# Weaving three weight slabs by token tile at each layer-norm boundary, and moving two weight and stream transfers to SyncE's queue

## The reference

```python
for l in range(DEPTH):                       # 2 layers
    proj = x @ w_in[l]                       # 1024 -> 5400 columns, feeds three mixers
    y_ssm, y_pool, y_nsa = ...               # state-space scan, causal pooling, sparse attention
    branch_d = einsum('bskc,kcd->bskd', branches, w_branch[l])
    merged = sum(sigmoid(br_g) * branch_d, axis=2)
    x = layer_norm(ALPHA * x + merged @ w_out[l], ln_g[l, 0], ln_b[l, 0])
    h_gate, h_up = split(x @ ffn_w_in[l], 2, axis=-1)
    x = layer_norm(ALPHA * x + (silu(h_gate) * h_up) @ ffn_w_out[l], ln_g[l, 1], ln_b[l, 1])
```

## Time and profile before

| what | value |
|---|---|
| median of three runs | 1762.86 us (1762.06 to 1764.96) |
| the profiled execution's own time | 1763.78 us |
| its span, first to last instruction | 1762.0 us |
| PE busy | 1731.0 us, 98% of the span |
| DVE / ACT / POOL busy | 53% / 37% / 7% |
| mean granted TensorE clock | 0.998 of full speed |
| DMA, mean | 99 GB/s |

### The profile page before, as it was taken

One profiled execution on the slowest core, in us unless ns is written; L12 is line 12 of the kernel. 1 busy time (PEld: TensorE's weight loads), 2 busy tenths in 40 slices (PEclk: granted clock), 3 DMA queues, 4 the chain that ended last, 5 costly groups with the idle time before them and its releaser, 6 DMA issues.

```text
span 1762.0 us, 26801 instructions
## 1 busy us (share of the span) xinstructions
PE 1731.0 (98%) x10172; PEld 1408.2 (80%) x10172; DVE 940.7 (53%) x1514; ACT 650.5 (37%) x1152; POOL 128.2 (7%) x252
## 2 busy tenths in 40 slices
PE   7999999999999999999999999999999999999998
PEld 7778777788888888888887777777888888888886
DVE  5788777545354444422358877865453544444223
ACT  4333666422242222221353346664222522222112
POOL 4710000000000000000047000000000000000000
PEclk9999999999999999999999999999999999999999
DMA  7543111122422222222263331111233222222222
GB/s 261 165 110 89 54 49 49 59 98 100 165 72 96 95 95 96 100 95 92 97 242 117 107 88 60 43 49 67 93 118 118 84 96 95 95 95 95 96 96 84
DMA packets 65918, 174.88 MB, mean 99 GB/s; under 512 B 14256, under 2 KB 26576, under 8 KB 65056
## 3 DMA queue, kind: packets, MB, share of 16 engines
q1 hardware_dynamic: 40192, 140.53, 23.2%
q10 hardware_dynamic: 21888, 13.64, 3.2%
q0 software_dynamic: 3744, 19.41, 3.1%
HBM read 162.27 MB, written 7.08 MB: 96 GB/s over the span
## 4 chain that ended last, share of the span: by engine, by line
PE 92%; DVE 4%; DVEq 2%; ACT 1%; issue 1%; DMA 0%
PE ps L532 20%; PE ps L534 19%; PE ps L533 19%; PE ps L570 6%; PE ps L572 6%; PE ps L571 6%; PE ps L857 2%; PE ps L844 2%; PE ps L830 2%; PE ps L550 1%; PE ps L673 1%; PE ps L561 1%; PE ps L551 1%; PE ps L552 1%; DVE wlo L1376 1%; PE ps L833 1%
## 5 line engine op out<-in xcount | busy, mean ns | idle before, releaser
L532 PE MATMUL ps<-xh,whi 128*128 128x512 f32 x1312 | 520.7, 397 | 5.7 <-DVE wlo L1376 3.4
L534 PE MATMUL ps<-xh,wlo 128*128 128x512 f32 x1312 | 512.0, 390 | 0.0
L533 PE MATMUL ps<-xl,whi 128*128 128x512 f32 x1312 | 511.5, 390 | 0.0
L1376 DVE TENSOR_TENSOR wlo<-raw,whi 128x1024 fp32r<-128x1024 f32 x264 | 324.1, 1228 | 348.4 <-ACT whi L977 339.1
L977 ACT ACTIVATE whi<-raw 128x1024 fp32r<-128x1024 f32 x264 | 278.7, 1056 | 349.2 <-PE ps L572 234.2
L532 PEld LDWEIGHTS ps<-xh,whi 128*128 128x128 f32 x1312 | 246.7, 188 | 57.4 <-DVE wlo L1376 5.1
L534 PEld LDWEIGHTS ps<-xh,wlo 128*128 128x128 f32 x1312 | 246.6, 188 | 52.6
L533 PEld LDWEIGHTS ps<-xl,whi 128*128 128x128 f32 x1312 | 247.0, 188 | 49.1 <-issue 0.5
L570 PE MATMUL ps<-whi,hh 128*128 128x512 f32 x352 | 137.5, 391 | 0.0
L572 PE MATMUL ps<-whi,hl 128*128 128x512 f32 x352 | 137.0, 389 | 0.0
L571 PE MATMUL ps<-wlo,hh 128*128 128x512 f32 x352 | 137.0, 389 | 0.0
(11 more groups left out here) (338 smaller groups left out, 2331.2 us busy)
## 6 DMA issues: line engine op xcount, KB each, us to landing
raw<-wstream SPq DMA_DIRECT2D x264, 512.0 KB, 3.2
w<-w1s POOLq DMA_DIRECT2D x4, 2048.0 KB, 11.7
sm<-smalls POOLq DMA_DIRECT2D x2, 1060.0 KB, 7.1
xt<-xin ACTq DMA_DIRECT2D x4, 512.0 KB, 6.4
scratch_u<-pa ACTq DMA_DIRECT2D x8, 256.0 KB
toep<-scratch_k ACTq DMA_DIRECT2D x4, 512.0 KB
toep_b<-scratch_k ACTq DMA_DIRECT2D x4, 512.0 KB
xt<-xin POOLq DMA_DIRECT2D x4, 512.0 KB, 4.1
```

Source lines behind the costliest of these rows:

```text
L532: pe.matmul(ps[:, bank, :], wh, hi[:, k, :], start=first and i == 0, stop=False)
L533: pe.matmul(ps[:, bank, :], wh, lo[:, k, :], start=False, stop=False)
L534: m = pe.matmul(ps[:, bank, :], wl, hi[:, k, :], start=False, stop=last and i == len(blocks) - 1)
L1376: dve.tensor_tensor(wlo[:, c % 2, :], raw[:, c % 2, :], whi[:, c % 2, :].bitcast(f32), SUB).then_inc(lo_ready, 1)
```

## The change

The last three slabs of an output stage, b-2, b-1 and b, are woven by tile, where it was two. PE's order is now: the three slabs for t = 0, 1; the three for t = 2; b-2 for t = 3; `turn_back` of the first half; b-1 and b for t = 3. Slab b and the next stage's first two slabs b+1, b+2 are split into three new buffers `whi_end`, `wlo_end`, laid over the start of `gates`/`hh`, so they no longer wait for the two ordinary slots; the new stage's third and fourth slabs, b+3 and b+4, are split inside `ln_part` too. `first_pair` starts when both its slabs are split, turns the second half in the middle of the second slab, and alternates the two slabs on the second token half. Layer 0 keeps its old start (`first_slabs`). In the norm DVE normalizes columns 0-511 in both halves, and takes the statistics of tile 3 after three of the four groups of `halves`. The w1 load is cut into 8 pieces of 512 KB per layer, and with the save of x (4 x 512 KB) it is issued by SP between the slab loads of the layer's first slabs instead of by POOL.

```diff
+    whi_end = place("whi_end", big_at, [P, 3, 1024], f32r)
+    wlo_end = place("wlo_end", big_at + 3072, [P, 3, 1024], f32r)
...
-            with sp.Fori(0, L * NSLAB // 2 - 1) as h:
...
+            def load_w1(l, m):
+                j, part = m // 4, slice(1024 * (m % 4), 1024 * (m % 4) + 1024)
+                sp.dma_start(w1[:, j, part], w1s[l * 2 + j, :, part]).then_inc(w1_in[j], 16)
+            for l in range(L):
+                for c in range(8):
+                    load_slab(l * NSLAB + c, c % 2)
+                    if c == 2 and l:
+                        sp.wait_ge(ln_x, l * 16)
+                    if c in (2, 3) and l:
+                        for t in (2 * c - 4, 2 * c - 3):
+                            sp.dma_start(scr_x[:, t, :], xt[:, t, :]).then_inc(x_stored, 16)
+                    if c == 3:
+                        sp.wait_ge(slab_done, l * NSLAB + 4)
+                    if c in (3, 4, 5, 6):
+                        load_w1(l, 2 * c - 6)
+                        load_w1(l, 2 * c - 5)
+                with sp.Fori(0, NSLAB // 2 - 4 - (l == L - 1)) as h:
...
-                if l:
-                    wait(slab_done, l * NSLAB + 2)
-                    load_w1()
-                if l:
-                    wait(ln_x, l * 16)
-                    for t in range(4):
-                        pool.dma_start(scr_x[:, t, :], xt[:, t, :]).then_inc(x_stored, 16)
...
-                if l == 0:
-                    wait(slab_done, 4)
-                    load_w1()
...
+                for s in range(3):
+                    pe.wait_ge(lo_ready, b - 2 + s + 3)
+                    for t in (0, 1):
+                        m = token_products(ends[s][0], ends[s][1], 1, t, k + 2 * s, hi, lo, s == 2)
+                        if s == 2:
+                            m.then_inc(t_psum, 1)
+                for s in range(3):
+                    m = token_products(ends[s][0], ends[s][1], 1, 2, k + 2 * s, hi, lo, s == 2)
+                m.then_inc(t_psum, 1)
+                token_products(ends[0][0], ends[0][1], 1, 3, k, hi, lo, False).then_inc(slab_done, 1)
                 turn_back(n, 0, rt)
-                token_products(b % 2, 1, 3, k + 2, hi, lo, True).then_inc(slab_done, 1)
+                for s in (1, 2):
+                    token_products(ends[s][0], ends[s][1], 1, 3, k + 2 * s, hi, lo, s == 2).then_inc(slab_done, 1)
...
             def first_pair(n, at, rt):
-                pe.wait_ge(lo_ready, at + 3)
+                pe.wait_ge(lo_ready, at + 4)
                 for g in range(4):
                     x_quarter(at, 0, g, n * 8)
-                if n:
-                    turn_back(n - 1, 1, rt)
-                pe.wait_ge(lo_ready, at + 4)
+                for g in (0, 1):
+                    x_quarter(at + 1, 0, g, n * 8)
+                turn_back(n - 1, 1, rt)
+                for g in (2, 3):
+                    x_quarter(at + 1, 0, g, n * 8)
                 for g in range(4):
-                    x_quarter(at + 1, 0, g, n * 8)
-                for c in range(2):
-                    for g in range(4):
+                    for c in range(2):
                         m = x_quarter(at + c, 1, g, n * 8)
...
+            def split_end_hi(c, slot, free):
+                act.wait_ge(raw_loaded[c % 2], (c // 2 + 1) * 16)
+                act.wait_ge(slab_done, free + 3)
+                act.activation(whi_end[:, slot, :], raw[:, c % 2, :], ACT.Copy).then_inc(hi_ready, 1)
+            def stage_splits(at, pairs, last):
+                b = at + 2 * pairs - 1
+                split_end_hi(b, 0, b - 3)
+                if not last:
+                    split_end_hi(b + 1, 1, b - 3)
...
                 for t in (2 * half, 2 * half + 1):
-                    for fh in (0, 1) if half and n < 2 * L - 1 else (1,):
```

More of the change, by code:

```diff
@@ L592, in to_tokens @@
                     residual(n, fh)
-                    for s in range(pairs - 2 * fh):
+                    for s in range(pairs - 3 * fh):
                         c = at + fh * pairs + s
@@ L598, in to_tokens @@
                         for t in range(4):
-                            m = token_products(c % 2, fh, t, 2 * s, hi, lo, fh == 0 and s == pairs - 1)
+                            m = token_products(whi[:, c % 2, :], wlo[:, c % 2, :], fh, t, 2 * s, hi, lo, fh == 0 and s == pairs - 1)
                         m.then_inc(slab_done, 1)
-                a, b = at + 2 * pairs - 2, at + 2 * pairs - 1
-                k = 2 * pairs - 4
-                pe.wait_ge(lo_ready, a + 3)
-                for t in (0, 1):
-                    token_products(a % 2, 1, t, k, hi, lo, False)
@@ new lines, in to_tokens @@
+                ends = ((whi[:, (b - 2) % 2, :], wlo[:, (b - 2) % 2, :]), (whi[:, (b - 1) % 2, :], wlo[:, (b - 1) % 2, :]), (whi_end[:, 0, :], wlo_end[:, 0, :]))
+                k = 2 * pairs - 6
+                for s in range(3):
[4 more added lines that the diff above has]
+                            m.then_inc(t_psum, 1)
@@ L1014, in ln_part @@
                 if not last:
-                    split_hi(0, next_slab)
+                    split_end_hi(next_slab + 1, 2, next_slab - 4)
                 for g in range(4):
                     gained(n, 0, g, rt, last)
+                if not last:
+                    split_next_hi(next_slab + 2, next_slab - 2)
                 deviations(n, 1)
-                if not last:
-                    split_hi(0, next_slab + 1)
                 normalized(n, 1, rt)
@@ L1023, in ln_part @@
                     gained(n, 1, g, rt, last)
+                if not last:
+                    split_next_hi(next_slab + 3, next_slab - 2)
             def x_part(buf, q):
@@ L1344, in _ @@
                         merged_hi(c // 5 - 1)
-                for c in range(1, NO):
+                for c in range(1, NO - 1):
                     split_hi(0, l * NSLAB + OO + c)
@@ L1348, in _ @@
                         merged_hi(3)
+                stage_splits(l * NSLAB + OO, KD // 2, False)
                 ln_part(l * 2, l * NSLAB + OF, xt)
@@ L1352, in ff_pairs @@
                     for c in range(4):
-                        if not (first and c == 0):
+                        if not first or c == 3:
                             split_hi(h, c + 1)
@@ L1365, in _ @@
                     ff_pairs(hl_ + OF // 2 + 2 + i * 2, i + 1, False)
-                for c in range(1, NG):
+                for c in range(1, NG - 1):
                     split_hi(0, l * NSLAB + OG + c)
+                stage_splits(l * NSLAB + OG, KF // 2, l == L - 1)
                 ln_part(l * 2 + 1, (l + 1) * NSLAB, xt)
@@ L1491, in ln_part @@
                 first_columns(0)
+                if not last:
+                    split_end_lo(next_slab + 1, 2)
                 second_stats(n, 2, next_slab + 2)
-                if not last:
-                    split_lo(0, next_slab)
-                halves(n, 0, 0, rt, last)
-                if last:
-                    halves(n, 0, 1, rt, last)
+                for g in range(3):
+                    halves(n, 0, g, rt, last)
                 second_stats(n, 3, next_slab + 2)
                 variances(1)
+                if not last:
+                    halves(n, 0, 3, rt, last)
+                scalars(n, 1)
+                first_columns(1)
                 if last:
-                    scalars(n, 1)
-                    first_columns(1)
                     halves(n, 0, 3, rt, last)
                 else:
-                    halves(n, 0, 1, rt, last)
-                    scalars(n, 1)
-                    for g in (2, 3):
-                        halves(n, 0, g, rt, last)
-                    split_lo(0, next_slab + 1)
+                    split_lo(0, next_slab + 2)
                 for g in range(4):
                     halves(n, 1, g, rt, last)
+                if not last:
+                    split_lo(0, next_slab + 3)
             dve.memset(tiny[:, 0:1], 0.0).then_inc(lo_ready, 2)
@@ L1957, in _, with stage @@
                         x.then_inc(mg_raw, 1)
-                def stage(at, pairs, last_low=False):
-                    for c in range(1, 2 * pairs):
+                def stage(at, pairs, last_low=False, last=False):
+                    b = at + 2 * pairs - 1
+                    for c in range(1, 2 * pairs - 1):
                         if c == pairs + 1:
@@ L1965, in stage @@
                             low_parts(3)
+                    split_end_lo(b, 0)
+                    if not last:
+                        split_end_lo(b + 1, 1)
                 stage(l * NSLAB + OO, KD // 2, True)
@@ L1991, in _ @@
                     ff_pairs(hl_ + OF // 2 + 2 + i * 2, i + 1, False)
-                stage(l * NSLAB + OG, KF // 2)
+                stage(l * NSLAB + OG, KF // 2, last=l == L - 1)
                 ln_part(l * 2 + 1, (l + 1) * NSLAB, xt)
```

76 lines of the change are left out of this document (46 added, 30 removed).

## The result

The kernel after takes **1750.35 us** (median of 4 runs, 1749.6 to 1750.73). Beside it the kernel before takes 1762.82 (4 runs, 1762.06 to 1764.96). The ratio is 0.9926, 95% interval 0.9914 to 0.9938: faster by 12.5 us. The forecast was 1754.6 and its range began at 1750.5. That nearness is a coincidence: C wanted every wait gone, and a third of the quarter waits stayed. The profiled execution of after took 1750.73 us with a span of 1748.6, against 1763.78 and 1762.0 before, so the spans differ by 13.4.

The account below looks back on a forecast made before the run. PE bounds the kernel, busy 1731.0 of 1762.0 us. 1763.78 less 6.3 (boundaries) and 2.0 (w1 and x off POOL) gives 1755.5; that execution lies 0.92 above the median, so 1754.6 us, range 1750.5 to 1759.5.

Parts of the forecast that it names:

- C: Rival for the whole kernel: every wait goes, 9.5 and 3.4 us gained, 1750.0 us; chance 0.06.
- The boundaries: Output-stage ends n = 0, 1, 2: 2.3, 2.0 and 2.0 us gained, 6.3 together; bounds 3 and 9.5.
- margins of 1.2 and 0.6: At a boundary: us to spare between normalized columns and the first turn_back (1.2), and the second half's turn (0.6).
- 3.1 us lost at n = 1: Boundary n = 1 before: 34.74 us taken against 31.65 of pure PE work; 1.0 was to remain.
- n = 3: Last stage end: PE's work to the last product and what follows stay the same; zero, within 0.3 us.
- SP's queue: Slab loads with w1 and x pieces between: 286 GB/s needed against 359 seen, so costed at zero.
- Rival D: SP's transfers don't overlap, slabs slip 4.1 us in each of four intervals per layer; slower, 1782 us; chance 0.05.
- The state-space stage: With w1 and x off POOL the powers start earlier; 2.0 us gained over both layers, bounds 3.4 and -2.
- 1.7 of 1.93: Layer 0's PE wait of 1.93 us at 95.20: 1.7 gained as POOL's powers end near 78.
- a shift of 7: Layer 1: powers start some 7 us earlier against PE, still over most DVE operations; 0.3 of 1.44 us gained.
- The bounds: State-space term: at best 3.4 us (both waits gone), at worst -2 (slowdown lands on something PE wants sooner).
- The rule of exclusion: Two-input DVE and SBUF-reading GpSimd instructions exclude one another; moving POOL's work would gain 0 where DVE is busy throughout.

Follow-up runs that it names:

- e9: The kernel after with two slabs woven by tile instead of three at every stage end; 1756.72 us, ratio 0.9960 to before.
- e8: The kernel after with the second norm half's first 512 columns normalized by ACT again instead of DVE; 1754.04 us, ratio 0.9945 to before.
- e10: The kernel after with quarter products reordered: groups 0 to 2 of both slabs, second turn_back, then group 3 of both; 1750.50 us, ratio 0.9925 to before.
- e7: The kernel after with PE held before one slab of layer 0, an idle of 2.94 us; 1753.57 us, ratio 0.9940 to before.
- e4: The kernel after with POOL made to hold the powers back as long as its own transfers had held it; 1757.43 us, ratio 0.9964 to before.
- e3: The kernel before with only w1 moved to SyncE's queue, x still on POOL; 1759.23 us, ratio 0.9971 to before.
- e11: The kernel after with group 3 last and slab b+2 also split ahead of the first norm; 1754.69 us, ratio 0.9947 to before.
- e2: The kernel before with the new output stages, w1 and x left on POOL, w1 loaded behind x in layer 1; 1764.12 us, ratio 1.0000.
- e5: The kernel before with the last two doublings of POOL's powers only filled with zeros; 1758.21 us, ratio 0.9968 to before.
- e1: The kernel before with only the transfers of w1 and x moved to SyncE's queue; 1760.34 us, ratio 0.9978 to before.

## Why the prediction came out short

- **The boundaries** (forecast 6.3, measured 6.96): right in mechanism, place and nearly in size. The wait left is on group 3, no turn_back waits, and the margins of 1.2 and 0.6 came out as 1.0 (columns done at 867.73, turn_back at 868.74) and 0.5. e9 and e8 show that the woven slab and DVE's columns both carry the gain. The prediction had taken the 3.1 us lost at n = 1 from starts, where the brackets show 1.96, and that is why this term held. In e10 the wait moves to the second turn_back (1.0 us in all instead of 2.1), released by ACT's columns. What bounds the rest is not shown.
- **n = 3, SP's queue, x**: zero each, as forecast. Rival D is out: PE waits for no slab there, though a 512 KB piece takes 7.2 us from issue to landing. The slabs' median is 3.2 as before, but the three issued between the pieces of layer 0 (31.9, 38.1, 42.7) take 5.1 to 6.1. Beside POOL's 2 MB transfers two slabs had taken 10.2 and 9.5:

```profile
w<-w1s SPq DMA_DIRECT2D x16, 512.0 KB, 7.2
```

- **The state-space stage** (forecast 2.0, measured 6.3): the step that failed. "In layer 0 I take 1.7 of 1.93": the wait was priced well, but not the clock behind it, 1.6 us more, in which PE counts as busy. The page's clock digits stand for slices of 44 us, in which 3.4 us don't show. e7 and e4 reproduce the loss. "In layer 1 a shift of 7 leaves POOL over most of the same operations: I take 0.3 of 1.44": wrong. POOL's last instruction started 67.0 us behind the third slab before (962.53 - 895.49) and starts 55.5 behind it after (943.25 - 887.79), a shift of 11.6: the powers start 7.8 earlier and take 52.3 us instead of 56.1. And the loss there was not 1.44 but 3.06, with 1.05 in a stop that the prediction put at nothing. It also misread where POOL stood. Of the six operations of layer 1 only the first two are slow in before, because POOL was done at 962.66:

```profile
959.90 1.61 DVE L1382 TENSOR_TENSOR ta<-lam,bch 128x512 f32<-128x512 f32 x1
961.43 1.52 DVE L1382 TENSOR_TENSOR tb<-lam,bch 128x512 f32<-128x512 f32 x1
963.03 0.69 DVE L1382 TENSOR_TENSOR vmat_b<-ta,tb 128x512 f32<-128x512 f32 x1
```

So even the shift of 7 would have left POOL over none of them. e3 shows the whole gain with w1 alone.
- **The bounds** were drawn from the two waits (3.4). That took a wait's length for its price. With 1.6 and 1.6 more (the clock, and layer 1's other stops) the bound of this term would have been 6.6, and the range would have reached below the time measured.
- **The rule of exclusion**: DVE's slow operations were indeed moved and not removed (1.54 at 67.48, 2.31 at 75.00). The gain wasn't 0, because it moved to where DVE is not what PE waits for next.

What stays open: the stop within the product L742, which comes with late powers (before 1.05, e4 1.36) and has no releaser in the profile; what decides between half and full clock at idles near 2 us; and how often the clock falls at such a place, since each kernel has one profiled execution.

## What to carry to other kernels

Price a stop from the starts on either side of it, not from its bracket. A wait of the bounding engine can be worth more than its length: look at the granted clock in a window behind each wait, count the matmuls started in it, and put the result into the bound. Where a helper slows the main engine, as POOL did DVE here, the gain can come from *when* the helper runs: put its work where the main engine has slack, and keep DMA issues of megabytes off its queue when they stand in front of that work. When a stage end is woven, count what stands behind the transposition as well as ahead of it.

## What the runs showed of the hardware

- A short idle of PE can be followed by half its granted clock: with 1.93, 2.87 and 2.94 us it was (before, e4, e7; 0.50 for about 3.4 us, and 1.6 us lost in before and e7), with 0.33, 1.00, 1.81 (e11, n = 1) and 1.98 (e2) it was not. The broken waits of the old boundary n = 1 (0.24, 1.28 and 0.44 us in e5) came with it in e1 and e5, 1.1 to 1.2 us more each time, and not in before and e3 with the same code there.
- DVE operations of 512 columns with two SBUF inputs took 1.37 to 1.78 us instead of 0.69 beside POOL's reading ones of 512 columns, a remainder 2.31 instead of 1.23. Beside POOL's of 128 columns they took 0.74 to 0.89 (before, 66.5 to 69). Filling memory from POOL did not slow them (e5).
- POOL stood idle for 13.9 us behind two issues of 2 MB and 8.9 behind four of 512 KB.
